# Wide and narrow products in turn, and 128 columns a bank for the mixers' query and key columns

## The reference

```
x = x + 0.5 * swiglu(rms_norm(x), w_gate, w_up, w_down)      # width 2816
x = x + hybrid_mixer(rms_norm(x), w_in, ...)                 # MLA, causal and dilated attention, gated and merged
x = x + 0.5 * swiglu(rms_norm(x), w_gate, w_up, w_down)
```

## Time and profile before

| | us |
|---|---|
| median of 3 runs (2813.65 to 2814.78) | 2813.79 |
| the profiled execution, its own time | 2814.14 |
| its span, first to last instruction | 2812.3 |
| TensorE matmul busy in the span | 2792.6 (99%) |
| TensorE weight load busy | 2396.6 (85%) |
| VectorE busy | 1921.3 (68%) |
| ScalarE busy | 1554.0 (55%) |

### The profile page before, as it was taken

The page is one execution under the profiler, slowest core; times in us unless marked ns, Lnnn a source line. Parts: engine busy times, 40 slices in busy tenths (PEclk is TensorE's granted clock), DMA queues, the critical chain, the costliest instruction groups (busy, mean ns, idle before and its releaser), DMA issues.

```text
span 2812.3 us, 40293 instructions
## 1 busy us (share of the span) xinstructions
PE 2792.6 (99%) x15556; PEld 2396.6 (85%) x15556; DVE 1921.3 (68%) x3180; ACT 1554.0 (55%) x2718; POOL 241.5 (9%) x187
## 2 busy tenths in 40 slices
PE   9999999999999999999999999999999999999998
PEld 8889888888889888888888987888888888878887
DVE  6756676747655667756568777776566687777765
ACT  6545656545545656545456556455455465655553
POOL 0010011010010011010014100110100141001100
PEclk9999999999999999999999999999999999999999
DMA  6544445555544345555554344555555554445553
GB/s 242 191 171 158 149 156 182 193 185 190 195 167 152 139 172 194 199 190 195 195 193 179 136 163 159 210 194 182 199 189 195 183 187 153 158 156 184 209 185 135
DMA packets 75055, 503.82 MB, mean 179 GB/s; under 512 B 8784, under 2 KB 10480, under 8 KB 19184
## 3 DMA queue, kind: packets, MB, share of 16 engines
q1 hardware_dynamic: 74576, 501.07, 50.2%
q10 hardware_dynamic: 288, 0.17, 0.0%
HBM read 500.12 MB, written 1.08 MB: 178 GB/s over the span
## 4 chain that ended last, share of the span: by engine, by line
PE 93%; DVE 4%; POOL 2%; issue 1%; ACT 1%; DMA 0%; SPq 0%; DVEq 0%; ACTq 0%
PE ps L1544 45%; PE ps L1579 21%; PE ps L1585 11%; PE ps L1563 9%; PE ps L1606 3%; POOL wlo L2498 2%; DVE wlo L2038 1%; PE ps L1701 1%; PE ps L1699 1%; DVE conv L2327 1%; PE ps L1726 1%; PE ps L1716 0%; PE ps L1717 0%; PE ps L1718 0%; DVE ps L2144 0%
## 5 line engine op out<-in xcount | busy, mean ns | idle before, releaser
L1777 ACT ACTIVATE whi<-raw 128x1024 fp32r<-128x1024 f32 (+3 forms) x938 | 977.5, 1045 | 600.3 <-PE ps L1544 426.1
L2038 DVE TENSOR_TENSOR wlo<-raw,whi 128x1024 fp32r<-128x1024 f32 (+2 forms) x894 | 1084.1, 1220 | 219.9 <-ACT whi L1777 218.9
L1579 PE MATMUL ps<-xT_both,whi 128*128 128x512 f32 x2560 | 641.6, 393 | 0.0
L1544 PE MATMUL ps<-whi,xT_both 128*128 128x512 f32 (+2 forms) x2336 | 628.9, 391 | 2.6 <-DVE xT_both L2061 1.6
L1579 PEld LDWEIGHTS ps<-xT_both,whi 128*128 128x128 f32 x2560 | 461.1, 189 | 82.6
L1544 PEld LDWEIGHTS ps<-whi,xT_both 128*128 128x128 f32 x2336 | 425.5, 188 | 83.7 <-issue 9.3
L1585 PEld LDWEIGHTS ps<-xT_both,wlo 128*128 128x128 f32 x2560 | 349.3, 191 | 24.9
L1585 PE MATMUL ps<-xT_both,wlo 128*128 128x256 f32 x2560 | 357.1, 282 | 0.0
L1544 PE MATMUL ps<-wlo,xT_both 128*128 128x512 f32 (+2 forms) x1168 | 354.6, 385 | 0.3 <-DVE wlo L2038 0.3
L2118 DVE TENSOR_TENSOR h<-h,ps 128x256 f32<-128x256 f32 x320 | 127.0, 418 | 203.1 <-ACT h L1826 203.1
L1544 PEld LDWEIGHTS ps<-wlo,xT_both 128*128 128x128 f32 x1168 | 218.4, 188 | 43.7 <-DVE wlo L2038 1.4
(11 more groups left out here) (315 smaller groups left out, 2526.7 us busy)
## 6 DMA issues: line engine op xcount, KB each, us to landing
raw<-in_w SPq DMA_DIRECT2D x435, 1024.0 KB, 4.8
vr<-in_vrows SPq DMA_DIRECT2D x19, 512.0 KB, 5.6
raw<-in_w SPq DMA_DIRECT2D x12, 768.0 KB, 4.3
raw<-in_w SPq DMA_DIRECT2D x10, 896.0 KB, 4.5
sums<-scratch SPq DMA_DIRECT2D x8, 512.0 KB, 4.4
raw<-in_w SPq DMA_DIRECT2D x4, 832.0 KB, 4.4
raw<-in_w SPq DMA_DIRECT2D x4, 576.0 KB, 3.7
raw<-in_w SPq DMA_DIRECT2D x4, 512.0 KB, 6.9
```

Of the source, the lines that this page charges most:

```text
L1544: made = e.matmul(bank[:, 0:c1 - c0], xs[:, kt, sl], ws[:, j * w + c0:j * w + c1], start=kt == 0 and n == 0, stop=kt == job.nk - 1 and n == 2)
L1579: e.matmul(bank[:, :].rearrange("p (n x) -> p n x", n=2), hi[:, o:o + 128], job.xt.both[:, :, kt, :], start=kt == 0, stop=False, skip_grou ...
L1777: e.activation(out, raw, ACT.Copy).then_inc(*mark("hi", i))
L2038: e.tensor_tensor(out, raw, hi.bitcast(F32), sub).then_inc(*mark("lo", i))
```

## The change

Two parts.

1. In `wide` the narrow product of a block follows its wide product at once, on the same bank. The wait for `wlo` stands before the first narrow product, so it comes after one wide product of the piece where it came after eight.
2. The first mixer's query and key columns (18 blocks of 128 a layer) and the second's `qc` and `kc` (16 blocks a layer together) take the form `wide`: one block a bank, chunks of two blocks and two pieces where they had four blocks and four pieces. A new step `parts_out` empties each bank: ScalarE copies the second half to SBUF, then VectorE adds the first half. `xbc` stays in the form `columns`. The count of pieces stays 938, and the loads stay as they were.

```diff
@@ plan
-            gemm(("qk1", l, c), (l,), 8, QK1[c])
+            for a in (2 * c, 2 * c + 1):
+                gemm(("qk1", l, a), (l,), 8, QK1[a])
...
-        gemm(("qk1", l, 4), (l,), 8, QK1[4])
+        gemm(("qk1", l, 8), (l,), 8, QK1[8])
...
-        for key, at in (("qa", QA), ("ka", KA), ("va", VA), ("qc", QC), ("kc", KC), ("vc", VC)):
-            for n in (0, 1):
-                gemm((key, l, n), (l,), 8, [(w, at + 512 * n, at + 512 * n + 512)])
+        for key, at, c in (("qa", QA, 512), ("ka", KA, 512), ("va", VA, 512), ("qc", QC, 256), ("kc", KC, 256),
+                           ("vc", VC, 512)):
+            for n in range(1024 // c):
+                gemm((key, l, n), (l,), 8, [(w, at + c * n, at + c * n + c)])
@@ mixer1
+            for a in (2 * c, 2 * c + 1)[0:9 - 2 * c]:
+                banks, free = self.two()
+                tok = self.gemm_w(("qk1", l, a), xt, 8, banks, free, "wide")
+                for j, b in enumerate(banks):
+                    qk_there[2 * a + j] = ("copy_v", "qk", l, 2 * a + j)
+                    self.do("parts_out", qk_there[2 * a + j], qk[:, 2 * a + j, :], b, (tok,))
+                    self.main.put(b, qk_there[2 * a + j])
@@ mixer2
-            outs = [banks[i // 2][:, 256 * (i % 2):256 * (i % 2) + 256] for i in range(4)]
-            tok = self.gemm_w((name, l, n), xt, 8, outs, free)
+            tok = self.gemm_w((name, l, n), xt, 8, banks, free, "wide")
...
-        for n in (0, 1):
+        for n in range(4):
             qkc_chunk("qc", n, 0)
-        for n in (0, 1):
+        for n in range(4):
             qkc_chunk("kc", n, 8)
@@ wide
                 e.matmul(bank[:, :].rearrange("p (n x) -> p n x", n=2), hi[:, o:o + 128], job.xt.both[:, :, kt, :],
                          start=kt == 0, stop=False, skip_group_check=True)
-        pe.wait_ge(*at(*lo_there))
-        for j, (_, kt, _) in enumerate(kts):
-            for c, bank in enumerate(job.outs):
-                o = j * w + 128 * c
+                pe.wait_ge(*at(*lo_there))
                 made = e.matmul(bank[:, 256:512], lo[:, o:o + 128], job.H[:, kt, :], start=False,
                                 stop=kt == job.nk - 1, skip_group_check=True)
@@ scalar_program
+    def parts_out(there, out, bank, after):
+        for f in after:
+            act.wait_ge(*at(*f))
+        e.activation(out, bank[:, 256:512], ACT.Copy).then_inc(*mark("copy_a", "part", *there[1:]))
@@ vector_program
+    def parts_out(there, out, bank, _):
+        dve.wait_ge(*at("copy_a", "part", *there[1:]))
+        e.tensor_tensor(out, out, bank[:, 0:256], add).then_inc(*mark(*there))
```

More of the change, by code:

```diff
@@ L94 @@
 _Q = [("w_in", 416 + 128 * i) for i in range(6)] + [("w_in", 1568 + 128 * i) for i in range(12)]
-QK1 = [[(n, c, c + 128) for n, c in _Q[4 * i:4 * i + 4]] for i in range(5)]
+QK1 = [[(n, c, c + 128) for n, c in _Q[2 * i:2 * i + 2]] for i in range(9)]
 COLS = {}
@@ L1270, in qkc_chunk @@
             banks, free = self.two()
-            outs = [banks[i // 2][:, 256 * (i % 2):256 * (i % 2) + 256] for i in range(4)]
-            tok = self.gemm_w((name, l, n), xt, 8, outs, free)
+            tok = self.gemm_w((name, l, n), xt, 8, banks, free, "wide")
             for j in (0, 1):
[L1274 to L1278, removed]
-        for n in (0, 1):
+                hh = base + 2 * n + j
+                self.do("parts_out", ("copy_v", "qkc", l, hh), qkc[:, hh, :], banks[j], (tok, *fence2))
+                self.main.put(banks[j], ("copy_v", "qkc", l, hh))
+        for n in range(4):
             qkc_chunk("qc", n, 0)
-        for n in (0, 1):
+        for n in range(4):
             qkc_chunk("kc", n, 8)
@@ L1290, in qkc_there @@
         def qkc_there(b):
-            return ("copy_a" if b % 4 > 1 else "copy_v", "qkc", l, b - b % 2)
+            return "copy_v", "qkc", l, b
         def heads_c():
@@ L2015, in scalar_program @@
         "scale_row": scale_row, "glu": glu, "halve_h": halve_h, "halve_o": halve_o,
-        "exps": exps, "turn_probs": turn_probs, "latents": latents, "bank_out": bank_out, "uq_out": uq_out,
+        "exps": exps, "turn_probs": turn_probs, "latents": latents, "bank_out": bank_out, "parts_out": parts_out, "uq_out": uq_out,
         "ukv_out": ukv_out, "mla_turn": mla_turn, "dil_weights": dil_weights, "gate1": gate1, "z_out": z_out,
@@ L2456, in vector_program @@
         "norm_probs": norm_probs, "o_out": o_out, "dil_weights": dil_weights, "dil_sum": dil_sum, "latents": latents,
-        "bank_out": bank_out, "uq_out": uq_out, "ukv_out": ukv_out, "merge": merge, "scalars": scalars,
+        "bank_out": bank_out, "parts_out": parts_out, "uq_out": uq_out, "ukv_out": ukv_out, "merge": merge, "scalars": scalars,
         "dt_soft": dt_soft, "dt_sums": dt_sums, "dt_turn": dt_turn, "conv_rest": conv_rest, "cb": cb,
```

## The result

The changed kernel takes 2822.07 us (median of 8 runs, 2821.81 to 2822.34), the kernel before 2814.02 on the same chip (8 runs, 2813.57 to 2814.78). The ratio is 1.0028, 95% interval 1.0017 to 1.0039: slower by 8.05 us, where I forecast 12 us faster. The profiled run took 2821.84, its span is 2820.0 (before: 2812.3), TensorE's granted clock 0.999 in both.

What follows compares the result with a forecast made beforehand. TensorE was taken as the bound, through the distances between its products. Part 1's -6.1, part 2's -7.2 and +1.5 us of lateness on the profiled 2814.14 gave 2802.3, forecast as a median of 2802.0 us, range 2785 to 2822.

Steps and rivals of the forecast that it cites:

- The bound: Whole kernel: TensorE, busy for 99% of the span, sets the time through the distances between its products.
- The pair: In `wide`, one wide and one narrow product in turn: 346.8 ns, saving 6.1 us over 320 FFN pieces.
- the law: TensorE products: 0.417 ns a column plus 13.3 ns a product, from steady runs of 256, 288 and 512 columns.
- The bounds, 341.8 and 355: Low and high end, in ns, for one wide and one narrow product in turn in `wide`.
- D: Rival, `wide` in all 388 pieces: every wide product behind a narrow one takes 235 ns; 2827.4 us, chance 0.18.
- E: The forecast's own case: the law holds for products in turn; 2802 us, range 2796 to 2810, chance 0.45.
- Part 2 without the pair: Mixers' 68 query and key pieces: each from 2.880 to 2.774 us as `wide`, 7.2 us saved.
- Rival A: In `wide`, products in turn gain nothing, 349.1 ns a pair; only query and key blocks pay, 5.9 us; 2809.4, chance 0.20.
- The lateness: Mixers: TensorE waits longer for emptied banks, 1.0 us after `ukv` and 0.5 in the heads; 1.5 us, bounds 0 and 6.
- The heads' 0.5 us: Heads, whose transposes wait for VectorE's `pr` for 1.0 us in all: 0.5 us added.
- `wlo` and the cover in `qc` and `kc`: Earlier wait for `wlo` costs nothing; in the second mixer VectorE is busy 54.6 of some 58 us, below TensorE.

Runs made afterwards that it cites:

- e6: Changed kernel with the narrow product made as wide as the wide one, 512 columns both, adding low x low; 3135.8 us.
- e1: Kernel before with only the new order in `wide`, wide and narrow products in turn, mixers' query and key columns as they were; 2824.67 us.
- e9: Changed kernel with one added product of 96 columns ahead of the second wide chunk of each of the eight FFNs; 2809.09 us.
- e2: Changed kernel with the old order in `wide`, eight wide then eight narrow products, query and key columns still as `wide`; 2810.39 us.
- e8: Changed kernel with one added product ahead of the second wide chunk of each FFN, 32 to 256 columns, another width in each; 2814.88 us.
- e11: Changed kernel with an added product of 96 columns ahead of wide chunks 2, 6, 10, 14 and 18 of every FFN; 2814.40 us.
- e12: Changed kernel with FFN narrow products of 64 to 256 columns, another width in each FFN, so not the same work; 2795.3 us, one run.
- e4: Changed kernel with two wide products, then two narrow ones, and so on; 2808.00 us.
- e5: Changed kernel with eight wide and eight narrow products, every second piece narrow first, so runs of 16 form across pieces; 2806.95 us.

## Why the prediction was wrong

**The bound and the accounting: right.** The time is the sum of the distances between products, and the table above finds the whole difference in the places that the change touches, to 0.2 us.

**The pair: wrong, and this is the step that failed.** "I take the law, 346.8 ns, since it lies between them and three widths obey it." The three widths were measured in runs of one width, and the sequence in turn had no instance. e6 shows that the law holds in turn as well when the widths are equal; with 512 and 256 a pair takes 353.3 in 367 pieces of 388. The bounds, 341.8 and 355, do hold it. So part 1 came to +10.8 us in place of -6.1 (e1: +10.4 alone). The same 6.5 ns on 47 of 68 pieces make 2.4 of the 2.8 us that part 2 is short (-4.4 in place of -7.2). 2802 plus the 16.9 and the 2.8 us is 2821.7.

**The rivals.** D's mechanism won, at about the size that it named: a wide product takes 237 ns on average in place of 235, the narrow one 117 in place of 120, and 353.3 is over the 350.6 from which it decides. What I held against it, that the excess may need a run of eight narrow products, is refuted: a single one costs less each time (7 ns net against 20), but there are eight of them in a piece, which loses 53 ns in place of 20. But D is not the whole: in 21 pieces, and behind e9's added product, the sequence runs at the law of E. My range ended where D costs 353, 0.07 us short of the time. I cut D in half there for want of a row; nothing in the trace spoke for its cheaper half.

**Part 2 without the pair: nearly right.** In runs of eight (e2) the blocks gain 5.3 us, where I had 7.2. I priced its piece at 2.774 us, though the FFN's same piece stood in the earlier trace rows with 2.793, which alone is 1.3 us. Rival A had the better price for it, 5.9 us.

**The lateness: right in size and, after `ukv`, in place.** It is 1.50 us in all, as forecast. After `ukv` 0.42 us a layer came where I had 0.5, by the path that I named: the copies and VectorE's additions, the low part and the `v_mla` copies behind them, then TensorE. The other 0.34 us a layer came after `uq`, where the same additions hold up VectorE's work on `uq`'s banks; I had not looked there. The heads' 0.5 us did not come. That the sum is right to the hundredth is luck: one place that I named is empty and one that I did not name fills it.

**`wlo` and the cover in `qc` and `kc`: right.** There is no wait for `wlo` at L1578 (idle 0.0) and none in the second mixer, where VectorE is busy for 52.8 of 58.9 us against the 54.6 of some 58 that I had.

## What to carry to other kernels

A distance per product measured in runs of one width holds only for such runs: when products of different widths come in turn, price the pair by an experiment of one piece's order before rewriting a planner around it, and try runs of two and longer ones beside it. When a gain is spread over thousands of equal steps, a forecast should hold both ends of the step's price in its range, since 6.5 ns were worth 20 us here.

## What was not expected of the hardware

- One instruction sequence has two steady speeds, 346.7 and 353.3 ns a pair, each held over nearly a whole FFN (37 pieces, 296 pairs). A single short product ahead moved TensorE from the slower to the faster in most FFNs, and one further on moved it back (e8, e9, e11). What exactly decides is open.
- A pair of 512 columns and anything from 64 to 160, each with its own load of 128 columns of weights, takes 340 to 342 ns, and its loads start 108 ns or more apart (e12): 64 columns cost as much as 160. The 108 ns are no floor for every load: in the same trace some loads of 128 columns for transposes start 56 to 60 ns behind the one before.
- The excess for each place where a wide run follows a narrow one is 7 ns behind 1 product (in the slower pattern), 3 behind 2, 13 behind 4, 20 behind 8 and 19 behind 16. So neither the shortest nor the old run of 8 is the best; 2 and 16 are (e4, e5).
